# A Block boundary between routing and the experts of a hybrid decoder kernel

## What is computed

```python
g_sel = argmax(t @ w_rg + b_rg)                     # one of 4 groups per token
top_w, top_i = top_k(softmax(e_logits[g_sel]), 2)   # 2 of its 4 experts
for e in range(16):
    he = silu(t @ w_gate[e]) * (t @ w_up[e])        # 1024 -> 512
    y = y + gates[:, e:e + 1] * (he @ w_down[e])    # 512 -> 1024
```

## Time and profile before

| | |
|---|---|
| median of 3 runs | 1600.13 us (1596.68 to 1601.51) |
| the profiled execution | 1596.68 us |
| its span | 1594.8 us |
| TensorE busy | 94% of the span |
| VectorE busy | 74% |
| ScalarE busy | 53% |
| GpSimd busy | 31% |

### The profile page before, as it was taken

One profiled execution on the slowest core, in us unless ns is written; L12 is line 12 of the kernel. 1 busy time (PEld: TensorE's weight loads), 2 busy tenths in 40 slices (PEclk: granted clock), 3 DMA queues, 4 the chain that ended last, 5 costly groups with the idle time before them and its releaser, 6 DMA issues. The chain is left out here.

```text
span 1594.8 us, 19849 instructions
## 1 busy us (share of the span) xinstructions
PE 1505.0 (94%) x6550; PEld 1044.8 (66%) x6550; DVE 1175.0 (74%) x1740; ACT 847.5 (53%) x1234; POOL 497.4 (31%) x220
## 2 busy tenths in 40 slices
PE   7999999999898999999799999999998999999996
PEld 3587565545577888777546865655455778887773
DVE  2697499641368999999847975985314699999997
ACT  4642323531447778778464513236215478778881
POOL 3043123100003655554532421321000046554444
PEclk9999989999989999999999999999998899999998
DMA  6243301324017999999651440103140289999995
GB/s 221 84 106 132 118 1 53 122 66 158 1 66 262 375 399 397 398 399 398 236 185 40 106 144 1 38 16 132 55 158 1 106 289 398 399 398 399 399 399 187
DMA packets 151482, 312.71 MB, mean 196 GB/s; under 512 B 33158, under 2 KB 46380, under 8 KB 151228
## 3 DMA queue, kind: packets, MB, share of 16 engines
q1 hardware_dynamic: 140300, 271.39, 47.1%
q0 software_dynamic: 6624, 24.12, 4.0%
q10 hardware_dynamic: 4496, 16.40, 2.6%
HBM read 287.76 MB, written 29.50 MB: 199 GB/s over the span
## 5 line engine op out<-in xcount | busy, mean ns | idle before, releaser
L1879 POOL TENSOR_TENSOR rest_w_down<-arena,head_w_down 128x2048 fp32r<-128x2048 f32 x30 | 183.4, 6113 | 201.3 <-ACT head_w_down L1285 201.3
L647 PE MATMUL ps<-hT,arena 128*128 128x512 f32 x352 | 161.4, 599 | 0.0
L1290 DVE TENSOR_TENSOR rest_w_down<-arena,head_w_down 128x2048 fp32r<-128x2048 f32 x30 | 148.7, 4956 | 16.5 <-ACT head_w_down L1285 16.4
L1290 DVE TENSOR_TENSOR rest_w_gate<-arena,head_w_gate 128x2048 fp32r<-128x2048 f32 x64 | 145.9, 2280 | 0.1
L1290 DVE TENSOR_TENSOR rest_w_up<-arena,head_w_up 128x2048 fp32r<-128x2048 f32 x64 | 143.7, 2282 | 0.8 <-DVE slot_tok L1817 0.7
L1285 ACT ACTIVATE head_w_gate<-arena 128x2048 fp32r<-128x2048 f32 x60 | 114.6, 1922 | 41.7 <-DMA arena<-in_w_gate 41.6
L1285 ACT ACTIVATE head_w_down<-arena 128x2048 fp32r<-128x2048 f32 x60 | 115.2, 1927 | 39.9 <-DMA arena<-in_w_down 39.3
L1285 ACT ACTIVATE head_w_up<-arena 128x2048 fp32r<-128x2048 f32 x64 | 122.0, 1944 | 8.8 <-DMA arena<-in_w_up 8.7
L1825 POOL DMA_INDIRECT xg<-hrows,slot_tok x2 | 5.5, 2740 | 383.7 <-DVE slot_tok L1817 383.7
L647 PEld LDWEIGHTS ps<-hT,arena 128*128 128x128 f32 x352 | 63.4, 191 | 68.5 <-issue 67.5
L1274 PE MATMUL ps<-head_w_gate,xg_head 128*128 128x512 f32 x256 | 104.9, 410 | 1.2 <-DVE xg_rest L1303 0.5
(11 more groups left out here) (338 smaller groups left out, 3370.7 us busy)
## 6 DMA issues: line engine op xcount, KB each, us to landing
arena<-in_w_gate SPq DMA_DIRECT2D x64, 1024.0 KB, 10.4
arena<-in_w_up SPq DMA_DIRECT2D x64, 1024.0 KB, 11.2
arena<-in_w_down SPq DMA_DIRECT2D x64, 1024.0 KB, 10.7
arena<-in_w_in SPq DMA_DIRECT2D x10, 1536.0 KB, 6.9
yrows<-yb ACTq DMA_DIRECT2D x30, 512.0 KB, 6.3
arena<-in_w_in SPq DMA_DIRECT2D x4, 2048.0 KB, 8.9
x<-in_x SPq DMA_DIRECT2D x8, 512.0 KB, 13.8
arena<-in_w_in SPq DMA_DIRECT2D x16, 256.0 KB, 5.0
```

The lines of the kernel that those rows point to most:

```text
L647: last = nc.tensor.matmul(ps[n % 2][0:width, :], w[:, c, col:col + width], hT[:, c, :], start=(c == 0), stop=(c == KD - 1))
L1290: nc.vector.tensor_tensor(wl[q][:, c, :], raw[q][:, c, :], wh[q][:, c, :].bitcast(F32), ALU.subtract).then_inc(s_split[q], 1)
L1879: nc.gpsimd.tensor_tensor(wl[2][:, c, :], raw[2][:, c, :], wh[2][:, c, :].bitcast(F32), ALU.subtract)\
```

## The change

The experts' bodies move from the second Block of a layer into a third one. The three waits for `slots_done` ahead of the loops of SP, TensorE and ScalarE are dropped, and the clearing of `mix_sems` goes from behind SP's loop to the start of SP's body. The helper functions move out by one level of indentation. All the rest of the two parts stays as it is.

```diff
@@ -1825,25 +1825,25 @@
-                def block_count(eng):
-                    return eng.value_load(blki[0:1, NBC:NBC + 1], min_val=MINB, max_val=MAXB)
-
-                def last_two_out(eng):
-
-                    return eng.value_load(blki[0:1, NBC + 1:NBC + 2], min_val=MINB - 1, max_val=MAXB - 1)
-
-                count.clear()
-
+            def block_count(eng):
+                return eng.value_load(blki[0:1, NBC:NBC + 1], min_val=MINB, max_val=MAXB)
+
+            def last_two_out(eng):
+
+                return eng.value_load(blki[0:1, NBC + 1:NBC + 2], min_val=MINB - 1, max_val=MAXB - 1)
+
+
+
+            count.clear()
+            with nc.Block() as block:
                 @block.sync
                 def _(sp):
+                    sp.sem_clear(numbers(mix_sems))
                     load_expert(sp, 1, 2, 1)
-                    sp.wait_ge(sN["slots_done"], 1)
                     with sp.Fori(1, last_two_out(sp)) as k:
                         load_expert(sp, 0, k + 2, k + 1)
                         load_expert(sp, 1, k + 2, k + 1)
                         load_expert(sp, 2, k + 1, k)
-
-                    sp.sem_clear(numbers(mix_sems))
                     last = block_count(sp)
@@ -1980,7 +1980,6 @@
                     gate_up(2)
-                    pe.wait_ge(sN["slots_done"], 1)
                     with pe.Fori(1, last_two_out(pe)) as k:
@@ -2041,7 +2040,6 @@
                     silu(2)
-                    act.wait_ge(sN["slots_done"], 1)
                     with act.Fori(1, last_two_out(act)) as k:
```

## The result

The changed kernel took 1615.29 us (median of 4 runs, 1608.38 to 1616.9) against 1600.2 us of the kernel before (4 runs): ratio 1.009, interval 1.0061 to 1.0117. Two later timings of the same kernel, beside more runs of before, gave 1.0074 (1.0041 to 1.0106) and 1.0058 (1.0031 to 1.0084). The forecast was 1601.6 us, between 1597.5 and 1608.5, with 0.23 on slower. It was wrong, and the cause is rival (C).

What follows compares the result with a forecast made beforehand. VectorE, busy throughout an expert-loop block, was taken as the bound, so a later line 1303 moves the loop. The new block costs 0.2 + 1.35, about +1.5 us, other parts 0: 1600.13 + 1.5 = 1601.6 us, range 1597.5 to 1608.5.

Steps and rivals of the forecast that it cites:

- rival (C): At the new Block's end GpSimd is held until its gather lands: +9.5 us (1609.6) or +17 (1617); chance 0.12.
- GpSimd's own way out of the block: After the gather's issue, GpSimd's leaving of the new block end: 0.3 us, between 0 and the gather's landing.
- the meeting's 0.55: At the new block end, all five engines must arrive; the cost when nobody is late was taken as 0.55 us.
- Nothing downstream that catches up: Expert loop: whatever starts VectorE later at its head moves the whole loop, with none of the delay recovered.
- rival (E): Expert loop falls into another step; changed offset between VectorE and loads gives back at most about 10 us (1590); chance 0.06.
- issue of the gather: GpSimd's gather before the new block end: issue takes 0.97 us with VectorE idle, bounded by 2.76 on the other side.
- (B): Rival at the seam: GpSimd's gather issue, line 1825, is still 2.7 us long; chance 0.17.
- priced at 0.2: VectorE's `gated` at the head of the expert loop: held back by TensorE's products by 0.2 us in each layer.
- 7.32 us for the 24 products: TensorE's products behind the new boundary: priced at 7.32 us in both layers, after some 2.7 us of added idleness.
- ScalarE's Silu and heads: ScalarE behind the new boundary: 5.5 us from 489.4, ending ahead of the turn; without that cover up to 5.5 us.
- SP's load: Expert 2's w_up load is issued about 2.9 us later, hidden; without cover up to 2.9 us a layer.
- The clear and the three waits: Moving the 0.20 us semaphore clear ahead of SP's load, and dropping the slots_done waits: 0 each.

Runs made afterwards that it cites:

- e3: Changed kernel without GpSimd's drain at the Block's end, but with GpSimd explicitly waiting for its gather's landing; 1615.44 us, 1.0072 to before.
- e4: Changed kernel with the first half of expert 2's w_up (1 MB) issued by SP before the Block's end, beside the gather; one run, 1616.67 us.
- e1: Changed kernel with GpSimd's drain left out where the routing's Block ends, the engines still meeting there; 1600.61 us, 0.9973 to before.
- e2: Changed kernel with each layer's first gather moved to the head of GpSimd's body in the new Block; 1.0004 to before.
- e7: Changed kernel, third Block kept, with the clear behind SP's loop again and the three slots_done waits put back; 1615.7 us, 1.0079 to before.
- e8: Kernel before, two bodies in one Block, with eight small gate operations of VectorE moved ahead of the second half of rest_w_up; 0.9988 to before.
- single boundaries: Changed kernel with its new Block boundary in one layer only, the other layer as in the kernel before; layer 0 alone 1.0041, layer 1 alone 1.0009.
- e12: Repeat of e8, the kernel before with eight small gate operations ahead of the second half of rest_w_up; 1600.67 us, 0.997 to before.

## Why the prediction was wrong

**The step that failed** is "GpSimd's own way out of the block", for which I took 0.3 us, "nearer the short end, because at no row does a GpSimd instruction wait for an earlier DMA of its own". That the rows showed no such wait was no evidence, since in none of them did a Block end with a gather in flight. The trace of the kernel before does hold such an end, outside those rows: where the layer's second Block ends, GpSimd's last work is eight indirect DMAs of line 333. The last of them in layer 0, and the DRAIN of that Block's end (780 to 812 us):

```profile
791.21 1.09 POOL L333 DMA_INDIRECT arena<-yrows,pair_slot  x1 [0.30 <-issue]
L1337 POOLq DRAIN  x1: 14051/14051/14051, 784.1 to 784.1; - x1
```

That DMA landed 5.9 us after its issue, at 797.1, and the DRAIN ends at 784.1 + 14.05 = 798.2, 5.9 us after the issue's end at 792.3. So rival (C) could have been read before the change was made. Measured in the changed kernel: from the issue's end at 493.17 to the restart at 496.97, less the meeting's 0.55, it is 3.25 us where 0.3 was taken, and it ends with the landing (the DRAIN's record, e3, e4). That is rival (C), which had a chance of 0.12.

**C's own working.** It had line 1303 4.1 and 5.35 us later. Against the earlier trace rows and slot_tok, the changed kernel has it 3.96 later in layer 0, and in layer 1 1306.81 - 1290.43 = 16.4 against 1288.95 - 1277.24 = 11.7, 4.7 later. In layer 0 that is near the price by luck, for two errors cancel: the landing took 4.5 us and not 5.5, and from the restart to line 1303 it is 507.91 - 496.97 = 10.94 us and not 9.99, because `gated` waited 0.94 us for TensorE. The landing was quicker with the w_up load no longer beside it; with half of that load back it was 5.9 (e4).

**"Nothing downstream that catches up"** was right in part. From block 2's line 1303 to block 16's it is 755.78 - 499.55 = 256.2 us in before and 763.31 - 507.91 = 255.4 in the changed kernel: the loop of before waits for loads some blocks later (from 600 to 760 us ScalarE waits 13.6 us for those of w_down, and VectorE 8.2 us for the heads made of them), and 0.8 us of the 4.0 come back, by the mechanism of rival (E). Means over the profiles of the table that wait for the landing (e3 with them, e4 left out) against the old seam: experts 0 314.5 against 311.8, experts 1 321.5 against 318.4 us. Together +5.8 us, 0.36%, of the 4.0 + 4.7 by which line 1303 moved. So (C)'s sum of +9.5 us, which lies near the timed excess, is not met by its own path alone.

**What was right.** The issue of the gather falls to 1.04 to 1.16 us with VectorE idle beside it (priced at 0.97), so (B), which had a line 1825 of 2.7 us, did not come about. The meeting of the engines adds 0.65 us to VectorE's gap in e1 and 0.70 - 0.36 = 0.34 in e2 (0.55). The products start at a granted clock of 0.50 behind the new boundary, from 497 to 501 us; the changed kernel's row of 497 to 502 us has 0.52:

```profile
497.00:502.00 5.00, 4.98 (x12) 3.98 (x13) 4.55 (x15) 4.99 (x4) 0.00 (x0) 0.52 0.52 143
```

That held `gated` back by 0.94 us (priced at 0.2), and by 1.59 in e1. The 0.2 rests on 7.32 us for the 24 products, layer 1's time in before (1287.09 - 2.30 - 1277.47, with a clock of 0.71 over their start); no run shows that the boundary's idleness brings that time, which was my estimate, and in the changed kernel they took 8.0 us (497.02 to 504.99) and 7.7 us (1296.17 to 1303.89). It does not take the long idleness (6.42 us here): in e1 TensorE had been idle for 1.57 us, and its clock was 0.50 from 491.8 to 496.8 us. In e2, after 1.26 us in layer 0, the clock stayed at 1.00; in layer 1, after 1.22 us, it was 0.50 from 1290.8 to 1293.0 us, and `gated` waited 0.22 us. ScalarE's Silu and heads and SP's load stayed hidden: line 1303 starts with no wait at 507.91. The clear and the three waits are worth nothing (e7). That the length of the gather's issue belongs to the tensor_tensor beside it, as the forecast read it from the earlier trace rows, holds in e8 against before: 1.16 us against 2.76, with the order of VectorE's operations as the only edit. The long issue in before ends 1.03 us after the tensor_tensor does, about the length of a short one. What in the tensor_tensor holds it up, no run here shows.

**What stays open.** The timed ratios of the changed kernel, e3 and e7, 1.0058 to 1.009, lie above the 1.0036 of the stages. Chance in the clock may hold some of it, and the mixer of layer 1 (+1.3 us, not told apart) some; 2 to 7 us I can't place. The single boundaries leave both readings open: 1.0041 for layer 0, where its stage gives 2.7 us or 0.17%, and 1.0009 for layer 1, where it gives 3.1 us or 0.20%.

## What to carry to other kernels

A Block's end was cheap in itself here (0.34 and 0.65 us more in VectorE's gap, e2 and e1) and dear with a DMA of GpSimd in flight: its drain of 4.84 us turned a gather that was hidden into a wait of all five engines (VectorE's gap 5.88 us instead of 0.36). A load that SP had in flight did not hold it (a DRAIN of 0.13 us, e4). Before a boundary is put in, look for DMAs that GpSimd has outstanding there, and either issue them behind the boundary (e2), or leave the drain out where a semaphore orders the data anyway (e1). What a drain costs can be read: the trace has its record, with its length, at the line of the Block, in a kernel that already has such an end too. And where a GpSimd DMA is on the path, keep VectorE's large tensor_tensor from starting just ahead of it (an issue of 1.16 us instead of 2.76); this gave the shortest experts' stages here (e8, e12), and 0.1 to 0.3% of the whole.

## What the runs showed of the hardware

- GpSimd's drain waited for the landing of its indirect DMA: 4.84, 4.51 and 6.27 us long with landings of 4.5, 4.2 and 5.9 us, 0.04 us with nothing in flight (e2). The engines restarted 0.4 to 0.5 us after the landing.
- SP's drain did not wait for its load: 0.13 us with a load in flight that landed 5 us later (e4).
- An issue of an indirect DMA took 1.04 to 1.16 us beside small operations or none, 2.65 to 2.77 when rest_w_up (a tensor_tensor of 2.29 us) had started 0.5 to 0.6 us before it, and 1.16 when that began 0.1 us after it (e1). In before, the gathers of the loop show the same: 26 of 28 start 0.27 or 0.28 us after a tensor_tensor of rest_w_gate and take 2.86 or 2.87 us, and the two beside line 1303 take 0.97. In all of these the issue is long where the tensor_tensor had started 0.27 to 0.6 us before it, and short where it had not.
- The gather of 128 rows of 4 KB landed 4.2 to 4.5 us after its issue in quiet. With loads beside it and a short issue it took 5.1 to 6.4 (1 MB in e4; the 2 MB of w_up in e1, e8 and e12), and 8.7 to 10.3 with the same 2 MB and the long issue.
- The time of layer 0's mixer differs by up to 7.6 us between executions, with no edit in it or ahead of it. TensorE's granted clock goes with it in part: 0.98 over the first 330 us in before (327.9 us), 0.97 in e2 (335.4).
